# Prompt dilated attention of a hybrid decoder step: rounds of five chunks instead of rounds of three and two

## The reference, cut to what matters

```python
A_PATTERNS = ((128, 1), (512, 4), (2048, 16))
...
def dilated_attention_prompt(q, k, v):
    b, t, h, hd = q.shape
    outs, lses = [], []
    for window, dil in A_PATTERNS:
        n_sub = t // dil
...
        o, lse = banded_attention(to_residue(q), to_residue(k), to_residue(v), window // dil)
...
    return merge_by_denominators(outs, lses)
```

## Time and profile before

| what | value |
|---|---|
| median of 3 runs | 1872.31 us |
| the profiled execution, its own time | 1872.26 us |
| its span, first to last instruction | 1870.5 us |
| busy share of the span: PE, PEld, DVE, ACT, POOL | 96, 80, 48, 38, 21% |
| instructions | 35705 |
| the dilated stage of the prompt: first PE instruction, first of the next stage | 345.5, 466.2 us |

### The profile page before, as it was taken

One profiled execution on the slowest core, in us unless ns is written; L12 is line 12 of the kernel. 1 busy time (PEld: TensorE's weight loads), 2 busy tenths in 40 slices (PEclk: granted clock), 3 DMA queues, 4 the chain that ended last, 5 costly groups with the idle time before them and its releaser, 6 DMA issues. The chain is left out here.

```text
span 1870.5 us, 35705 instructions
## 1 busy us (share of the span) xinstructions
PE 1796.5 (96%) x13758; PEld 1497.9 (80%) x13758; DVE 888.6 (48%) x2638; ACT 704.4 (38%) x1541; POOL 401.5 (21%) x576
## 2 busy tenths in 40 slices
PE   7999999999998999999999999999799999999898
PEld 6788788687875998888888787787588888888898
DVE  5322222587546445222422323323777878777534
ACT  5100000474333232000012323223777777777423
POOL 0000000000661000000004222221456556565100
PEclk9999999999897999999999999999899999999899
DMA  6443434554879663744335241443400000000564
GB/s 215 149 152 129 170 134 135 191 165 135 281 233 300 218 215 126 221 159 165 125 86 201 94 152 57 156 143 120 131 19 25 24 25 16 15 14 13 187 190 151
DMA packets 158606, 254.11 MB, mean 136 GB/s; under 512 B 33867, under 2 KB 109896, under 8 KB 154088
## 3 DMA queue, kind: packets, MB, share of 16 engines
q1 hardware_dynamic: 143976, 206.02, 33.9%
q0 software_dynamic: 4608, 33.56, 4.9%
q10 hardware_dynamic: 9856, 12.26, 2.3%
HBM read 205.88 MB, written 52.96 MB: 138 GB/s over the span
## 5 line engine op out<-in xcount | busy, mean ns | idle before, releaser
L1837 POOL TENSOR_SCALAR sparse_pr<-sparse_pr,sparse_coef,sparse_gate 128x63 f32<-128x63 f32 (+8 forms) x384 | 245.6, 658 | 177.1 <-DVE sparse_coef L1787 177.1
L1112 PE MATMUL x_acc<-x_w_hi,x_y_lo 128*128 128x478 f32 (+3 forms) x768 | 273.4, 356 | 2.3 <-DVE x_y_lo L960 2.2
L1112 PE MATMUL x_acc<-x_w_lo,x_y_hi 128*128 128x478 f32 (+3 forms) x768 | 269.4, 351 | 0.0
L1112 PE MATMUL x_acc<-x_w_hi,x_y_hi 128*128 128x478 f32 (+3 forms) x768 | 269.0, 350 | 0.0
L1726 ACT ACTIVATE sparse_pr<-sparse_pr,sparse_nmax 128x63 f32<-128x63 f32 (+8 forms) x384 | 227.6, 595 | 75.5 <-DVE sparse_nmax L1781 75.5
L488 PE MATMUL h_acc<-h_w_hi,h_y_lo 128*128 128x512 f32 x448 | 176.7, 394 | 0.8 <-DVE h_y_lo L413 0.8
L488 PE MATMUL h_acc<-h_w_lo,h_y_hi 128*128 128x512 f32 x448 | 175.0, 391 | 0.0
L488 PE MATMUL h_acc<-h_w_hi,h_y_hi 128*128 128x512 f32 x448 | 174.8, 390 | 0.0
L1112 PEld LDWEIGHTS x_acc<-x_w_hi,x_y_lo 128*128 128x128 f32 x768 | 146.0, 190 | 22.0 <-issue 7.1
L1112 PEld LDWEIGHTS x_acc<-x_w_hi,x_y_hi 128*128 128x128 f32 x768 | 146.0, 190 | 11.2
L1112 PEld LDWEIGHTS x_acc<-x_w_lo,x_y_hi 128*128 128x128 f32 x768 | 146.2, 190 | 10.6
(11 more groups left out here) (397 smaller groups left out, 3052.6 us busy)
## 6 DMA issues: line engine op xcount, KB each, us to landing
h<-cmp_w SPq DMA_DIRECT2D x56, 256.0 KB, 2.1
h_w_side<-in_even_w_in SPq DMA_DIRECT2D x16, 896.0 KB, 6.1
h_w_raw<-in_even_w_in SPq DMA_DIRECT2D x6, 2048.0 KB, 8.2
x_w_side<-in_odd_w_in SPq DMA_DIRECT2D x16, 716.0 KB, 5.7
cmp_lent<-in_odd_w_in SPq DMA_DIRECT2D x5, 1912.0 KB, 8.8
h<-x_out SPq DMA_DIRECT2D x40, 239.0 KB, 2.4
ev_unit<-in_cache_a_k SPq DMA_DIRECT2D x4, 2048.0 KB, 10.0
ev_unit<-in_cache_a_v SPq DMA_DIRECT2D x4, 2048.0 KB, 12.3
```

The costliest lines, as they stand in the source:

```text
L1112: last = nc.tensor.matmul(acc[b][:, 0:passes[p][3]], left[:, k, t * P:(t + 1) * P], weights(right, p)[:, k, :], start=(k == 0 and a == 0), ...
L1837: nc.gpsimd.tensor_scalar(row, row, one, gate[:, t, 2 * i + e, (br + 1) % 3:(br + 1) % 3 + 1], ALU.mult, ALU.mult).then_inc(scaled, 1)
```

## The change

The dilated call gets the sparse call's order. One round holds the five chunks of a half pair. The distance from scores to turn is two rounds, which is again two half pairs. EXP_AFTER is gone: the exponentials of a round's units come in the round of their masks. Their coefficients move from behind the masks of a step to ahead of the masks of the next round. There are 10 buffers of turned probabilities and 40 places in `pr`; the ring of seven banks stays.

```diff
-    AHEAD = 3 if sparse else 4
-    EXP_AFTER = 0 if sparse else 1
-    N_T = 10 if sparse else 6
-    ROUNDS = {9: (5, 4), 10: (5, 5)} if sparse else {5: (3, 2)}
-    SLOTS = 68 if sparse else 44
+    AHEAD = 3 if sparse else 2
+    N_T = 10
+    ROUNDS = {9: (5, 4), 10: (5, 5)} if sparse else {5: (5,)}
+    SLOTS = 68 if sparse else 40
...
         k = step_of[last_chunk[u]]
-        exps[k + EXP_AFTER].append(u)
-        assert step_of[first_chunk[u]] + AHEAD >= k + 2 + EXP_AFTER
+        exps[k].append(u)
+        assert step_of[first_chunk[u]] + AHEAD >= k + 2
...
                     for g in outs[k]:
                         take(dve, "out", g)
-                    for u in exps[k - 1] if sparse and k else []:
+                    for u in exps[k - 1] if k else []:
                         coef_unit(u)
                     for c in fronts[k]:
                         mask_chunk(c)
                     if sparse and k == 1:
                         open_gates()
-                    for u in exps[k] if not sparse else []:
-                        coef_unit(u)
```

## The result

The changed kernel takes 1876.01 us in the median of 20 runs (1874.21 to 1879.47), the kernel before 1872.64 us in 20 runs beside it. The ratio is 1.0017, with a 95% interval of 1.0010 to 1.0023: 3.2 us slower, between 1.9 and 4.3. A second comparison, with 11 runs of the changed kernel, gave 1.0023 (1.0014 to 1.0032). The forecast was 1874.0 us, +1.8 on the profiled execution. The ratios leave out single executions that took far longer than all others (3248 us, one of the 20 of the kernel before). The first profiled execution of the changed kernel has a span of 1876.0 us against 1870.5.

A forecast was written before the change was run, and what follows sets the result against it. PE was taken to bound the dilated stage (busy 115.1 of 122 us), with DVE near. Terms -3.7 - 0.2 + 4.3 + 2.1 - 0.7 = +1.8 us on 1872.26 gave 1874.0 us, range 1868.5 to 1878.5.

The forecast's parts named there:

- the likeliest case: Whole kernel: ring waits and fill eat the gain of the long stretches, 1874.0 us, own range 1872 to 1876.5; chance 0.45.
- Merged stretches: PE in the dilated stage: each kind of work begun once instead of twice per half pair, saving 0.58 us each, -3.7 us.
- the rival by which a change of kind costs nothing: PE's switches don't come cheaper, while ring waits and fill are paid: +5.7 us, 1878 us; chance 0.15.
- The ring: PE's last score chunks wait for masked banks of the same round, 0.55 us (even) or 1.05 (odd): +4.3 us over five rounds.
- The rest as a whole: Stage without its fill: merged stretches -3.7, fewer prep switches -0.2, waits for banks +4.3, drain -0.7 us.
- The drain: Stage's end on PE: two 0.44 us waits for turned copies go, 0.1 left in each of two rounds, -0.7 us.
- The fill: Stage's start: DVE waits 2.3 us for ACT's exponentials before the second half pair, so first values end later, +2.1 us.
- The clock: Rival: PE's idle time in the fill drops the clock to 1.2 GHz for 13 us, +4.5 on top, 1878.5 us; chance 0.15.
- a clock that leaves 1.00 inside the stage: Sign named in advance: if the clock leaves 1.00 inside the dilated stage, the prediction is wrong.
- The fast case: DVE's masks start early enough for the ring and the fill's lag is made good: -4.6 us, 1867.7 us; chance 0.12.
- the shift lost in the next stage: Next stage's start hangs on loads and clock periods that don't move, so nothing reaches the end: 1872.3 us; chance 0.13.

The follow-up runs named there:

- out_late: Changed kernel with the out's entries, transposes and scaling behind the round's scores and masks; ratio 1.0006 (0.9997 to 1.0015) to the kernel before.
- ring6: Changed kernel with a ring of six banks instead of seven in the dilated call; ratio 1.0041 (1.0027 to 1.0055) to the kernel before.
- coef_late: Changed kernel with the coefficients of the round before placed behind the masks in DVE's loop; ratio 1.0017 (1.0007 to 1.0027) to the kernel before.
- split_exps: Changed kernel with the exponentials of a half pair's last two units one round later; ratio 1.0012 (0.9997 to 1.0027) to the kernel before.
- small_rounds: Changed kernel's order of exponentials and coefficients, but rounds of three and two chunks and four rounds from scores to turn; ratio 1.0019 (1.0010 to 1.0028) to the kernel before.

## Why the prediction was right, and where not

**The size.** 1874.0 was forecast and 1876.0 measured, inside the range and at the edge of what I had called no change. The ratio's interval leaves out 1, so the small loss is real, and its sign was that of the likeliest case. At full clock the stage would carry +2.9 us where the sum had +1.8; what lies above that in the traces is the clock, which the sum did not hold. The terms' errors don't cancel: fill +0.4, all the others together +0.7.

**Merged stretches, -3.7 us.** The direction holds, and nearly the size. Values went from 4.23 to 4.08 us as forecast, turns from 4.14 to 3.93 to 3.99 where 3.90 was forecast, and scores from 2.79 + 1.49 = 4.28 to 4.08, seen where the ring does not interrupt them ("out_late", even). That is 0.50 to 0.56 of the 0.58 us for a half pair, and about -3.3 us for the stage (an estimate: 7 turns and values, 5 scores). So the rival by which a change of kind costs nothing, at 1878 us, is out: the same matmuls take less time in one stretch. Whether what went was PE's own cost of a change or a dependence that went with it is not shown, since no run changed the number of switches alone.

**The ring, +4.3 us.** Named and sized rightly: scores were longer by 1.10 us in odd and 0.61 in even rounds (forecast 1.05 and 0.55), 4.5 us in five rounds. The first mask starts 6.48 us into the round where 6.52 was worked out. "ring6", "coef_late" and "out_late" each move these waits. That the fourth chunk hardly waits and the fifth carries it is seen too. The 0.06 us that the prediction adds for the signal came from no row; with the 0.1 for starting again it makes 0.16, and from the end of the third bank's mask to PE's next chunk the trace shows 0.15.

**The rest as a whole.** Forecast -0.3 us (-3.7, -0.2, +4.3, -0.7), measured +0.4. Rounds last 13.3 and 13.7 to 13.8 us instead of 13.15 and 13.65: the turns are 0.03 to 0.09 us longer than worked out, and the waits 0.05. The drain is as forecast: two rounds of 8.60 us.

**The fill, +2.1 us.** This is the term whose mechanism was half right, and that its size came close is in part luck, since two waits of about the same length, DVE's and PE's for the prep banks, stand side by side: +2.5 us at full clock and +3.4 in three of four traces. I took DVE's wait for the exponentials, ahead of the coefficients, as its cause. The wait is there much as forecast: DVE starts the second half pair 8.31 us after the first mask, where 8.4 was worked out. But "coef_late" took it away and the fill did not move. The cause is ACT's order: the exponentials of four units stand ahead of the preps of the second round, and those of four more ahead of the first turned copies. I had counted both (0.2 us for the preps, an upper bound of +3 for the turned bank) as side effects. "split_exps" moves half of them behind the copies, and the fill's loss is gone. "small_rounds" shows that the loss comes with the new order also where the rounds are short.

**The clock.** As a rival I gave it 1878.5 us and 0.15, and I named a clock that leaves 1.00 inside the stage as a sign of being wrong. That sign came in three of four traces, so the prediction was wrong in leaving the clock out of its sum. It does fall in the fill, after the idle time that I named, but for 3.4 us and not for 13, and costs 0.9 us instead of 4.5. The price was taken from a stretch where PE had less to do; here it was busy through the fall, 28 score matmuls took 4.91 us instead of 3.32, and the waits behind them hid part of the difference. The fall at the head (+1.2 to 1.5 us) I had not thought of.

**The other rivals.** The fast case (1867.7) is out: neither ring waits nor fill were absorbed. Nor was the shift lost in the next stage: the spans of the four traces of each kernel differ by 4.4 us in the mean (1875.0 and 1870.6), the stage itself by 4.7.

## What to carry to other kernels

When an order is cut into longer rounds, count the buffers of a stretch against the ring: when one stretch of one kind opens more banks than the ring has (here 10 score banks in a ring of 7, where 4 or 6 had shown no wait), its last ones wait for the first ones of the same stretch, and what stands ahead of their release on the releasing engine (here an out's scaling and four reciprocals) becomes part of the critical path. Moving the out behind the masks won back 2.5 of the 4.5 us. A pipeline's fill can hang on the engine that does two kinds of work in a fixed order; look there for long work that isn't urgent (exponentials due two rounds later) ahead of short work that is (copies that free banks), and split it.

## What the runs showed of the hardware

The granted clock at the stage's head went, over 14 traces, with a few tenths of a microsecond in the time at which PE starts. With the gap of 2.3 us behind the projection the same in both cases, the 16 transposes of the first preps took 1.94 us at full clock in the seven traces in which they start by 345.58 us of the span, and 3.2 to 3.6 us, most of them with the clock at 1.2 GHz, in the seven in which they start from 345.79 us on. What sets the two apart is not shown. Two kernels whose stages are equal can differ by 1.2 to 2.2 us from the first transpose to the first mask by this alone, so that differences of a microsecond are better read from stretches of the trace than from whole times.
